# Summing products whose result is wanted as columns, and where they stand among the down products

## The reference, cut to what matters

```python
c_act = jax.nn.silu(c)
for layer in range(DEPTH):
    mod = jnp.einsum('bd,dn->bn', c_act, w_ada[layer]) + b_ada[layer]
    sh1, sc1, gt1, sh2, sc2, gt2 = [m[:, None, :] for m in jnp.split(mod, 6, axis=-1)]
    h = rms_norm_2(x, g_attn[layer]) * (1.0 + sc1) + sh1
    y = hybrid_mixer(h, ...)
    x = x + gt1 * y
    h = rms_norm_2(x, g_ffn[layer]) * (1.0 + sc2) + sh2
    ...
    x = x + gt2 * f
```

## Time and profile before

| | |
|---|---|
| median of three runs | 2603.66 us (2602.05 to 2604.84) |
| profiled execution | 2602.44 us, span 2600.7 us |
| TensorE busy | 2527.5 us, 97% |
| VectorE busy | 1401.7 us, 54% |
| mean granted TensorE clock | 0.996 |
| summing products (L1415) | 24, each two passes of 512 columns |

### The profile page before, as it was taken

The page is one execution under the profiler, slowest core; times in us unless marked ns, Lnnn a source line. Parts: engine busy times, 40 slices in busy tenths (PEclk is TensorE's granted clock), DMA queues, the critical chain, the costliest instruction groups (busy, mean ns, idle before and its releaser), DMA issues.

```text
span 2600.7 us, 44267 instructions
## 1 busy us (share of the span) xinstructions
PE 2527.5 (97%) x18060; PEld 1624.5 (62%) x18060; DVE 1401.7 (54%) x2954; ACT 435.8 (17%) x1195; POOL 192.2 (7%) x313
## 2 busy tenths in 40 slices
PE   8999999999999999999999999999999999999996
PEld 7964457697499444478954559945546445645462
DVE  6787554788887965647886656665630000001102
ACT  1201252110012023221101321101311110111010
POOL 4010100001000103000011100001100000000000
PEclk9999999999999999999999999999999999999998
DMA  9684423467656743335674424553469999999997
GB/s 301 218 298 149 160 98 130 154 211 253 221 187 220 260 156 136 102 102 194 212 273 131 140 75 163 171 168 112 178 251 361 415 415 416 416 416 415 410 416 304
DMA packets 304524, 611.58 MB, mean 235 GB/s; under 512 B 15804, under 2 KB 172640, under 8 KB 304192
## 3 DMA queue, kind: packets, MB, share of 16 engines
q1 hardware_dynamic: 287216, 550.80, 57.5%
q0 software_dynamic: 17104, 57.91, 6.8%
HBM read 605.11 MB, written 3.54 MB: 234 GB/s over the span
## 4 chain that ended last, share of the span: by engine, by line
PE 80%; DVE 9%; DMA 6%; issue 4%; SPq 1%; ACT 1%; POOL 0%; DVEq 0%; POOLq 0%; ACTq 0%
PE psum L1391 23%; PE psum L1547 14%; PE psum L1971 6%; PE psum L1590 5%; PE psum L1444 4%; PE psum L1279 4%; PE psum L1682 4%; PE psum L1233 4%; DMA xn<-in_w_ada 3%; PE psum L1883 2%; PE psum L1996 2%; PE psum L1337 2%; DVE proj L3093 1%; PE psum L1581 1%; PE psum L1504 1%
## 5 line engine op out<-in xcount | busy, mean ns | idle before, releaser
L3718 DVE SCALAR_TENSOR_TENSOR proj<-proj,psum 128x256 f32<-128x256 f32 (+1 forms) x63 | 24.9, 395 | 533.4 <-ACT proj L2458 533.4
L1391 PE MATMUL psum<-xT,ring 128*128 128x128 f32 x1600 | 195.0, 275 | 0.0
L1547 PE MATMUL psum<-ring,xT 128*32 128x512 f32 (+3 forms) x2112 | 192.5, 513 | 2.2 <-DMA ring<-in_w_exp_up 1.6
L1391 PEld LDWEIGHTS psum<-xT,ring 128*128 128x128 f32 x1600 | 187.7, 192 | 5.8 <-issue 5.5
L1971 PE MATMUL psum<-ring,xT 128*128 128x384 f32 (+1 forms) x448 | 156.2, 498 | 1.1 <-DVE xT L2693 1.1
L1547 PEld LDWEIGHTS psum<-ring,xT 128*32 128x32 f32 x2112 | 78.4, 110 | 104.7 <-issue 91.9
L3093 DVE SCALAR_TENSOR_TENSOR proj<-xn,cols,proj 128x512 f32<-128x512 f32 x168 | 126.1, 751 | 17.3 <-DMA xn<-in_w_ada 13.1
L1682 PE MATMUL psum<-ring,memT 128*128 128x512 f32 x256 | 118.2, 599 | 2.5 <-issue 2.4
L1971 PEld LDWEIGHTS psum<-ring,xT 128*128 128x128 f32 x448 | 80.9, 190 | 61.2 <-issue 10.8
L1032 POOL DMA_DIRECT2D xn<-in_w_ada x96 | 69.4, 724 | 671.2 <-DVE proj L3093 664.6
L1444 PE MATMUL psum<-ring,sp_rows 128*128 128x512 f32 x220 | 105.2, 592 | 0.0
(11 more groups left out here) (597 smaller groups left out, 4168.2 us busy)
## 6 DMA issues: line engine op xcount, KB each, us to landing
ring<-in_ffn_w_gu SPq DMA_DIRECT2D x80, 1024.0 KB, 7.3
xn<-in_w_ada POOLq DMA_DIRECT2D x96, 512.0 KB, 4.8
ring<-in_ffn_w_down SPq DMA_DIRECT2D x44, 1024.0 KB, 7.2
ring<-in_w_exp_down SPq DMA_DIRECT2D x39, 1024.0 KB, 16.5
ring<-in_w_exp_gate SPq DMA_DIRECT2D x63, 512.0 KB, 12.4
ring<-in_w_exp_up SPq DMA_DIRECT2D x63, 512.0 KB, 15.4
ring<-in_xa_w_kv SPq DMA_DIRECT2D x16, 1024.0 KB, 10.3
ring<-in_w_in SPq DMA_DIRECT2D x60, 256.0 KB, 3.9
```

What stands on the lines that cost most here:

```text
L1391: ins = mm(banks[bank][:, t * P:(t + 1) * P], weights(t)[:, k, :], tokens[:, k, :], start=(new and t == 0 and k == 0), stop=(k == 3), skip ...
L1547: ins = mm(o[:, :, o0:o1], xg[e % 2][:, k, 32 * g:32 * g + 32], w_[:, :, c0:c1], start=(k == 0 and n_ == 0), stop=(k == KT - 1), skip_grou ...
```

## The change

For shifts and scales the running sum becomes the weights, and one column of ones is what moves. Output partition 64 * half + q, column k is the sum of `ada_sum` column 8 q + k, so each of eight products takes every eighth column (64 of them) and writes one column of 64 partitions: the result stands as columns at once, the two halves in their own partitions. In the last half layer four more products of 128 neighbouring columns give the experts' order. VectorE's read is a copy of 64 x 8 numbers (and one of 128 x 4 in the last half layer); the masked products, the reductions and the addition of the halves are gone. Gates keep the large product. In the down steps every summing product, gates' too, stands after P4 instead of between P3 and P7. Nothing changes on the DMA queues, ScalarE and GpSimd.

```diff
--- before.py
+++ after.py
@@ -470,7 +470,7 @@
         mod_shift = sb("mod_shift", [P, 4, KT])
         ada_bias = sb("ada_bias", [P, 2, 6, KT])
         ada_gain = sb("ada_gain", [P, 4, KT])
-        ada_cols = sb("ada_cols", [P, 3, KT])
+        ada_cols = sb("ada_cols", [P, 2, KT])
 
         exp_bias = sb("exp_bias", [P, 2, KT])
         exp_gain = sb("exp_gain", [P, KT])
@@ -587,7 +587,6 @@
         squared = [xn, sp_rows[:, :, :, :].rearrange("p n h s -> p (n h s)").rearrange("p (b d) -> p b d", b=NB)]
         p1_copy, u2_rows, v_rows, w_rows = (t.rearrange("p k s -> p (k s)") for t in quarter)
         values = [pT[f][:, :, :].rearrange("p (t b) s -> p t b s", t=2) for f in range(2)]
-        own_columns = diff_o[:, 0, :]
 
         flatT = xT[:, :, :].rearrange("p k s -> p (k s)")
         xg = [flatT[:, i * D:i * D + KT * CAP].rearrange("p (k s) -> p k s", k=KT) for i in range(2)]
@@ -1412,7 +1411,15 @@
                         else:
 
                             pe.wait_ge(sm["ada_used"], N_ADA * st["ada"] + 4 * (2 * number + half + 1))
-                            ins = mm(banks[7][:, :], C("ones"), ada_sum, start=True, stop=True)
+                            one = C("ones")[:, 0:1]
+                            if number == 2:
+                                ins = mm(banks[7][:, :], C("ones"), ada_sum, start=True, stop=True)
+                            elif st["ada"] == 3:
+                                for k in range(4):
+                                    mm(banks[7][:, KT + k:KT + k + 1], ada_sum[:, k * P:(k + 1) * P], one, start=True, stop=True)
+                            if number < 2:
+                                for k in range(KT):
+                                    ins = mm(banks[7][64 * half:64 * half + 64, k:k + 1], ada_sum[:, k:512:KT], one, start=True, stop=True)
                         ins.then_inc(sm[f"{what}_psum"], 1)
 
                 def down(d, name):
@@ -1473,8 +1480,7 @@
                         down(d, name)
                         if d == 0 and name == "P2":
                             products(NSTEP - 1, "M4")
-                        if name == "P3":
-                            through_last_bank(NSTEP + d, 0)
+                    through_last_bank(NSTEP + d, 0)
                 for name in DOWN_PRODUCTS:
                     down(NSTEP - 2, name)
                     down(NSTEP - 1, name)
@@ -3109,28 +3115,22 @@
                     return
 
                 if i == 3:
-                    own = own_columns.rearrange("p (k q) -> p k q", k=4)
-                    link(V.tensor_tensor(own, banks[7][:, :].rearrange("p (k q) -> p k q", k=4),
-                                         ident.unsqueeze(1).to_broadcast([P, 4, P]), ALU.mult))
-                    link(V.tensor_reduce(ada_cols[:, 2, 4 * h:4 * h + 4], own, AX_X, ALU.add))
-                own = own_columns.rearrange("p (k q) -> p k q", k=KT)
-                V.tensor_tensor(own, banks[7][:, :].rearrange("p (q k) -> p k q", k=KT),
-                                ident[:, 64 * h:64 * h + 64].unsqueeze(1).to_broadcast([P, KT, 64]), ALU.mult).then_inc(sm["ada_evac"], 1)
-                dve.wait_ge(sm["ada_evac"], count)
-                link(V.tensor_reduce(ada_cols[:, h, :], own, AX_X, ALU.add))
+                    V.tensor_copy(ada_cols[:, 1, 4 * h:4 * h + 4], banks[7][:, KT:KT + 4])
+                half_rows = slice(64 * h, 64 * h + 64)
+                V.tensor_copy(ada_cols[half_rows, 0, :], banks[7][half_rows, 0:KT]).then_inc(sm["ada_evac"], 1)
                 if h == 0:
                     return
-                link(V.tensor_tensor(ada_cols[:, 0, :], ada_cols[:, 0, :], ada_cols[:, 1, :], ALU.add))
+                dve.wait_ge(sm["ada_evac"], count)
                 if which == 0:
                     V.tensor_tensor(mod_shift[:, i, :], ada_cols[:, 0, :], ada_bias[:, l, 3 * half, :], ALU.add)
                     if i == 3:
-                        V.tensor_tensor(exp_mod[:, 1, :], ada_cols[:, 2, :], exp_bias[:, 0, :], ALU.add)
+                        V.tensor_tensor(exp_mod[:, 1, :], ada_cols[:, 1, :], exp_bias[:, 0, :], ALU.add)
                 else:
                     link(V.scalar_tensor_tensor(mod_gain[:, i, :], ada_cols[:, 0, :], 1.0, ada_bias[:, l, 3 * half + 1, :],
                                                 ALU.add, ALU.add))
                     link(V.tensor_tensor(mod_gain[:, i, :], mod_gain[:, i, :], ada_gain[:, i, :], ALU.mult))
                     if i == 3:
-                        link(V.scalar_tensor_tensor(exp_mod[:, 0, :], ada_cols[:, 2, :], 1.0, exp_bias[:, 1, :], ALU.add, ALU.add))
+                        link(V.scalar_tensor_tensor(exp_mod[:, 0, :], ada_cols[:, 1, :], 1.0, exp_bias[:, 1, :], ALU.add, ALU.add))
                         link(V.tensor_tensor(exp_mod[:, 0, :], exp_mod[:, 0, :], exp_gain[:, :], ALU.mult))
 
             def ffn(st):
```

## The result

The changed kernel takes **2633.4 us** (median of 4 runs, 2630.1 to 2636.2) against 2604.3 of before on the same chip: a ratio of 1.0107, with a 95% interval of 1.0095 to 1.0119. It is 1.1% slower. The forecast was 2605.6 us with a range up to 2620, so the time is outside the range, on the slower side. The profiled execution took 2636.24 us, the longest of the four; its span is 33.7 us above that of before, where the medians differ by 29.1.

A forecast was written before the change was run, and what follows sets the result against it. TensorE, busy 97% of the span, was taken to bound the kernel. The move -7.5, small products +5.8 and extra products +3.6 gave +1.9 us, VectorE's savings counting nothing: 2605.6 us on the median, range 2600 to 2620.

The forecast's parts named there:

- What bounds the kernel, and the stalls: TensorE, busy 97% of the span, sets the time; stalls cost four down stages 8.4 us against a stall-free 71.85 us each.
- Part one, the move: Down steps: summing products meet TensorE two products (1.72 us) later behind P4, so nearly all stalls go: -7.5 us.
- that passes through the DMA of the next slots to turn 14 ... so it costs nothing: Turn 12: VectorE's running sum starts 0.9 us late, but TensorE reaches turn 14 later too, so no cost.
- Rival three: Stalls stay: the running sum's two-slot DMA chain sets stage ends, the move wins only half, -4; 2609 us, chance 0.08.
- Part three, VectorE's savings: Short copies save VectorE some 25 us, but TensorE doesn't wait for it there outside the down stages: 0 us taken.
- Part two, sixteen passes of 0.057 us: Shift and scale turns: 16 small passes take 0.91 us, a turn 1.22 against 0.86, +0.36 times 16: +5.8 us.
- The change of the array's shape: Around each small-product turn on TensorE: half-array use costs +0.10 us going in, +0.10 coming out, +0.11 for an unhidden load.
- Rival one: Small products' strided weight loads run at half speed, 0.111 us a pass, +14.0 us; 2619 us in all, chance 0.26.
- The extra products: Last stage: four turns get four more products of 128 weight columns, 0.89 us a turn: +3.6 us.
- I carry no clock term: Granted clock is 1.00, the 2.4 GHz level, in all five down stages, so no time was added for a slower clock.
- What would show it: Signs in the new profile: load times and durations, turns of 1.2 us, TensorE's waits near 0, stage lengths, turn 12's read.

## Why the prediction was wrong, point by point

**What bounds the kernel, and the stalls: right.** A stall-free stage of 71.85 us was read from rows and measures 71.88; the 8.4 us of stalls are real and are gone in the changed kernel.

**Part one, the move, -7.5 us: right for the stages of the changed kernel, wrong as a step.** With large products, the move and the copies the stages lose 7.3 us, but the median only 4.3 (2604.3 to 2600.0), so 3.2 of the 7.5 us didn't come. The step that failed is "that passes through the DMA of the next slots to turn 14 ... so it costs nothing". With the long read the lateness of turn 12 reaches the later turns and the weight sums, and the move costs 10.3 us. Only with the copies does the stage run free. Rival three named this chain and gave it too small a part; in the changed kernel the copies pay for it.

**Part three, VectorE's savings, 0 us: wrong in its reason.** The text asked whether TensorE waits for VectorE outside the down stages. Inside them the savings are worth 4.9 us in place and 14.6 behind P4. Most of that only undoes what the move does, so the sum was hurt little.

**Part two, sixteen passes of 0.057 us: wrong, the largest miss and the step that decided.** Measured: 0.120 us. The turn costs +1.34 us, not +0.36: 16 x 0.98 = 15.7 us more. The change of the array's shape, 0.10 in, 0.10 out and 0.11 for the exposed load, came out as forecast (0.09, 0.09 and 0.10), and with neighbouring columns the whole turn did. What failed is the choice that the loads would run as the earlier trace rows shows for neighbouring ones. Rival one had the right mechanism, at 0.26; its price (0.111) was 8% short, and the argument against it, that 188 and 192 ns are alike and so the stride's price hides in what a real product's load takes anyway, is refuted: the stride adds 0.060 us to a pass of 0.060. The rows on which it leaned were loads of 128 columns; here 64 strided columns take 217 ns, more than 128 neighbouring ones.

**The extra products, +3.6 us: near.** 2.12 - 1.34 = 0.78 us a turn, 0.89 forecast: 3.1 us, without their part in the spells.

**"I carry no clock term": wrong, the second step that failed.** It was taken from a kernel whose stages hold full-size products alone. With one-column products TensorE is busy in the profile and falls to 1.2 GHz all the same: 13.7 us in the profiled execution. Neither the forecast nor a rival had it. Rival one at 2619 us with the 1.6 us that its turns were short (16 x (1.34 - 0.36 - 0.88)) and these 13.7 would have been 2634. That this is so near 2633.4 is partly luck, since its -8.0 for the stalls is too much by the medians and 13.7 is from the longest of four executions.

**What would show it.** Loads within 0.9 us: no, the last starts 1.82 us after the first, as under rival one. Load durations of 137 ns: no, 216, beyond even the 190. No waits at the summing products: yes. Stages of 72.6, 72.9, 72.6 and 74.4 us: no, 74.6, 78.0, 74.6 and 79.5. VectorE's read at turn 12 about 2 us later in its stage: 2.9 us later (175.78 - 159.21 against 167.53 - 153.82), since the product ends later by the dearer passes too:

```profile
175.78 0.16 DVE L3120 COPY ada_cols<-psum 64x8 f32<-64x8 f32 x1 [4.01 <-PE psum L1422]
```

## What to carry to other kernels

Price a small product by its weight load, and look at how far apart in bytes its weight columns lie: here 8 bytes were free and 16 doubled the pass. Before a wait is moved later, look up how busy the engine that waits for the product is in that stage, not over the span; one that is 90% busy passes its lateness on through every slot that it has to free. And a turn that swaps a wide product for many one-column ones can cost its neighbours their clock, as some waits of over 2 us did here. The rows read from the kernel before showed neither.

## What the hardware showed that was not expected

- The weight load's pace as a step function of the columns' distance, for fp32 in two passes: 138 ns at 4 and 8 bytes, 217 ns at 16 and 32, for 64 columns.
- The clock fell to 1.2 GHz behind a stretch in which TensorE was busy without a gap by the profile, 5.00 of 5.00 us, part of it with one-column products; each spell was 3.4 or 6.8 us long and 3.4 us of it cost 1.7. "TensorE: Matmul & The Clock Gate" of the Trainium skill, Part 1, says of the gate that "activity releases the throttle"; here it was throttled behind rows that are busy for all of their time.
- Strided one-column passes are not slowed by the lower clock. In the run with 32 of them the clock had fallen at 183.3 us, and the passes went on to 184.63 at 0.120 us each, while the full products behind them took twice their time:

```profile
180.70 4.00 PE L1422 MATMUL psum<-cst,proj 128*64 128x1 f32 x32
184.63 3.78 PE L1451 MATMUL psum<-ring,proj 128*128 128x512 f32 x4
```

- Pieces of 512 KB that were asked for within 0.9 us of a load of 1 MB on the other queue took 7.4 to 7.9 us to land, in three places of one run; before, at the same places, asked for 1.7 to 2.2 us ahead of that load, they took 4.0 to 5.1. A slot freed 1.4 us later became 3.5 us of waiting.
